# Reordering the seams between the stages of a decoder layer on one core: first loads, table turns, the last stores of y, and who reads y

## What is computed

```python
u = rmsnorm(x, g_mix) @ w_in                     # 1024 -> 512, 32 groups of 16 channels
bu = einsum(u, bb)                               # complex, 64 states a group
s_t = lb * s_(t-1) + bu_t                        # scan over the tokens; samples start from s0
y = gelu(Re(C s) + d * u)                        # 512 wide
a = y @ w_out;  x2 = x + a[:, :1024] * sigmoid(a[:, 1024:])
h = rmsnorm(x2, g_ffn)                           # router: best of 4 groups, then 2 of its 4 experts
x3 = x2 + sum_k weight_k * (silu(h @ w_gate_k) * (h @ w_up_k)) @ w_down_k
out = rmsnorm(x3, g_final), the last state of each sequence
```

## Time and profile before

| | us |
|---|---|
| median of 3 runs (lowest, highest) | 881.96 (881.44, 885.02) |
| the profiled execution's own time | 882.48 |
| its span on the core | 880.7 |
| TensorE busy | 805.5 (91%) |
| VectorE busy | 598.2 (68%) |
| ScalarE busy | 409.0 (46%) |
| PoolE busy | 332.6 (38%) |

### The profile page before, as it was taken

One profiled execution on the slowest core, in us unless ns is written; L12 is line 12 of the kernel. 1 busy time (PEld: TensorE's weight loads), 2 busy tenths in 40 slices (PEclk: granted clock), 3 DMA queues, 4 the chain that ended last, 5 costly groups with the idle time before them and its releaser, 6 DMA issues.

```text
span 880.7 us, 14971 instructions
## 1 busy us (share of the span) xinstructions
PE 805.5 (91%) x4204; PEld 649.6 (74%) x4204; DVE 598.2 (68%) x1143; ACT 409.0 (46%) x737; POOL 332.6 (38%) x443
## 2 busy tenths in 40 slices
PE   4899998996899999999964999999999999999982
PEld 2788875555788888888743788888888888888861
DVE  5798769996333345535575678876867878876852
ACT  6456752123332443424221565764745755754630
POOL 3600001001200000060335257767777667766532
PEclk9899999999899999999975999999999999999996
DMA  7454314886842332423314857865877668876721
GB/s 241 159 212 171 143 18 100 244 179 127 299 144 94 121 137 79 144 93 125 109 26 131 318 207 259 262 231 190 281 250 250 225 232 302 282 254 221 283 90 74
DMA packets 57780, 160.93 MB, mean 183 GB/s; under 512 B 22480, under 2 KB 26960, under 8 KB 51024
## 3 DMA queue, kind: packets, MB, share of 16 engines
q1 hardware_dynamic: 34704, 112.70, 39.6%
q0 software_dynamic: 22976, 47.05, 15.1%
HBM read 128.75 MB, written 62.40 MB: 217 GB/s over the span
## 4 chain that ended last, share of the span: by engine, by line
PE 75%; DMA 7%; DVE 7%; issue 4%; SPq 2%; ACT 1%; POOL 1%; DVEq 0%; POOLq 0%; ACTq 0%
PE pbig L1219 8%; PE pbig L1215 8%; PE pbig L1216 8%; PE pbig L1125 7%; PE pbig L1127 6%; PE pbig L1126 6%; PE pbig L1240 4%; PE pbig L1242 4%; PE pbig L1241 4%; PE pbig L1203 4%; PE pbig L986 3%; PE pbig L988 3%; PE pbig L987 3%; PE pbig L1148 3%; DMA y_by_block<-U 3%
## 5 line engine op out<-in xcount | busy, mean ns | idle before, releaser
L1215 PE MATMUL pbig<-WH,xgH 128*128 x320 | 130.4, 407 | 1.4 <-ACT xgH L885 1.4
L1216 PE MATMUL pbig<-WL,xgH 128*128 x320 | 126.0, 394 | 0.0
L1125 PE MATMUL pbig<-w2H,ysH 128*128 128x512 f32 (+1 forms) x272 | 111.2, 409 | 8.5 <-DVE ysL L1545 8.5
L1127 PE MATMUL pbig<-w2H,ysL 128*128 128x512 f32 (+1 forms) x272 | 108.4, 399 | 0.0
L1126 PE MATMUL pbig<-w2L,ysH 128*128 128x512 f32 (+1 forms) x272 | 108.2, 398 | 0.0
L589 POOL DMA_INDIRECT x_sums<-xg,recs x36 | 81.9, 2276 | 39.3 <-DVE xg L1802 31.6
L1691 DVE SCALAR_TENSOR_TENSOR WL<-WR,gf_p,WH 128x512 f32 (+1 forms) x128 | 86.3, 746 | 5.0 <-ACT WH L851 3.1
L1581 DVE TENSOR_TENSOR x<-pbig,sg 128x1024 f32<-128x1024 f32 (+1 forms) x17 | 20.8, 1224 | 91.6 <-PE pbig L1127 91.2
L851 ACT ACTIVATE WH<-WR,gf_p 128x512 f32 (+1 forms) x128 | 80.5, 711 | 5.2 <-DMA WR<-in_w_gu 3.1
L1219 PE MATMUL pbig<-WH,xgL 128*128 x320 | 81.2, 395 | 0.0
L1802 DVE SCALAR_TENSOR_TENSOR xg<-pbig,recs,xg 128x1024 f32<-128x1024 f32 x40 | 51.2, 1281 | 34.6 <-PE pbig L1242 34.6
(11 more groups left out here) (287 smaller groups left out, 1741.8 us busy)
## 6 DMA issues: line engine op xcount, KB each, us to landing
WR<-in_w_gu SPq DMA_DIRECT2D x32, 1024.0 KB, 6.6
WR<-in_w_dn SPq DMA_DIRECT2D x16, 1024.0 KB, 6.0
xT<-in_x_cols SPq DMA_DIRECT2D x16, 512.0 KB, 3.5
low<-in_x_rows SPq DMA_DIRECT2D x16, 512.0 KB, 4.5
U<-in_x_rows SPq DMA_DIRECT2D x16, 512.0 KB, 5.1
x_mid<-x SPq DMA_DIRECT2D x16, 512.0 KB, 2.6
x_sums<-x SPq DMA_DIRECT2D x16, 512.0 KB, 3.9
w<-in_w_out SPq DMA_DIRECT2D x1, 4096.0 KB, 12.4
```

The source lines that it names most:

```text
L1125: pe.matmul(pbig[0:rows, n, :], ysH[b][:, k, 0:rows], w2H[n][:, k, :], start=(k == 0), stop=False)
L1127: mm = pe.matmul(pbig[0:rows, n, :], ysL[b][:, k, 0:rows], w2H[n][:, k, :], start=False, stop=(k == CB - 1))
L1215: pe.matmul(pbig[:, 6, :], xgH[b][:, k, :], WH[:, w], start=(k == 0), stop=False)
L1216: pe.matmul(pbig[:, 6, :], xgH[b][:, k, :], WL[:, w], start=False, stop=False)
```

## The change

The diff does six things. (1) The loads of the second and third `xT` come ahead of three small tables and of the first rows; ScalarE does `x_root(t)` in step t and not one step earlier; the eight small transfers of the samples are split four and four behind tiles 4 and 5, `a_spread(0)` moves from behind tile 2 to behind tile 6, and the tables `turn_table(5)` and `e_table` swap places. (2) The turns of `E` come three, three and two behind tiles 13, 14 and 15, over four banks. (3) The first two `b_state` go between the last fills, and ScalarE empties all of these but one. (4) The samples' states: ScalarE copies the raw values per step (`fo_raw`), VectorE adds all start states once behind the stage. (5) The stores and loads of the last quarter of y are issued crosswise, each store with its own semaphore. (6) `ys` and PoolE's copies are gone: ScalarE and VectorE read `U` and `ytail`; ScalarE's order of `w2_hi(3)` and `c_y_hi(0, 0)` changes.

```diff
             for k in range(KD):
                 sp.dma_start(w1[:, k, :], w_in[:, k, :]).then_inc(S[f"win{k}"], 16)
+            x_load(1)
             for dst_, src in ((BC[:, :, :, :], bc_in), (s0_sb[:, :, :, :], s0), (d_sb[:, :], d_in)):
                 sp.dma_start(dst_, src).then_inc(S["bc_in"], 16)
+            x_load(2)
             row_load(0)
-            x_load(1)
             row_load(1)
             sp.dma_start(gf_p[:, :], gffn).then_inc(S["rt_in"], 16)
             sp.dma_start(wr_sb[:, :, :], w_route).then_inc(S["rt_in"], 16)
             for t in range(2, TA):
-                x_load(t)
+                if t >= 3:
+                    x_load(t)
                 row_load(t)
-                if t == 2:
+                if t in (4, 5):
 
                     sp.wait_ge(S["us_done"], 1)
-                    for j in range(L):
+                    for j in range(4 * t - 16, 4 * t - 12):
                         sp.dma_start(us8[:, :, L - 1 - j, :], us[j * DECB:(j + 1) * DECB, :, 0, :]).then_inc(S["us8_in"], 16)
...
             cb = CB - 1
-            for q in range(4):
+
+            def tail_store(q):
                 sp.wait_ge(S["gelu_done"], 8 * cb + 2 * q + 2)
-                sp.dma_start(yD[cb][:, 2 * q:2 * q + 2, :], U[:, cb * 8 + 2 * q:cb * 8 + 2 * q + 2, :]).then_inc(S["y_stored"], 16)
-                if q == 0:
-                    sp.wait_ge(S["tabs_ready"], 1)
-                    sp.wait_ge(S["wt_small"], 1)
-                    sp.wait_ge(S["k_done"], 1)
-                sp.wait_ge(S["y_stored"], 16 * (cb + q + 1))
+                sp.dma_start(yD[cb][:, 2 * q:2 * q + 2, :], U[:, cb * 8 + 2 * q:cb * 8 + 2 * q + 2, :]).then_inc(S[f"yt_st{q}"], 16)
+
+            def tail_load(q):
+                sp.wait_ge(S[f"yt_st{q}"], 16)
                 for g in (2 * q, 2 * q + 1):
                     sp.dma_start(ytail[g * GC:(g + 1) * GC, :, :],
                                  yD[cb].rearrange("(i c) g k -> g c i k", c=GC)[g]).then_inc(S["y_tail"], 16)
+
+            tail_store(0)
+            tail_store(1)
+            sp.wait_ge(S["tabs_ready"], 1)
+            sp.wait_ge(S["wt_small"], 1)
+            sp.wait_ge(S["k_done"], 1)
+            tail_load(0)
+            tail_store(2)
+            tail_load(1)
+            tail_store(3)
+            tail_load(2)
+            tail_load(3)
             sp.wait_ge(S["fo_done"], 2 * PR)
+            sp.wait_ge(S["fo_sum"], 1)
             sp.dma_start(st_out, FO[:, :, :, :]).then_inc(S["st_stored"], 16)
...
-            def c_copy(t, part):
...
-                    pool.tensor_copy(ys[b][:, 0:CB - 1, 0:rows], yflat[:, 0:CB - 1, t * P:t * P + rows]).then_inc(S["ys_done"], 1)
...
             x_hi(1)
-            x_root(0)
-            x_root(1)
             for t in range(TA):
                 if 1 <= t < TA - 1:
                     x_hi(t + 1)
-                    x_root(t + 1)
-                if t == 3:
+                x_root(t)
+                if t == 7:
                     spread(0)
                 if t in (L + 2, L + 3):
...
                 if t > TURN_AT:
-                    turned(2 * (t - 1 - TURN_AT))
-                    turned(2 * (t - 1 - TURN_AT) + 1)
+                    for f in range(3 * (t - 1 - TURN_AT), min(3 * (t - TURN_AT), PR // 2)):
+                        turned(f)
             x_scale(TA - 1)
-            turned(PR // 2 - 2)
-            turned(PR // 2 - 1)
-            for q in range(10, FILLS, 2):
+            for q in range(10, FILLS):
                 spread(q)
...
             def c_y_hi(t, part):
                 b, rows = t % 2, P if t < TF else LAST
-                act.wait_ge(S["ys_done"], 2 * t + part + 1)
+                if t == 0 and part == 0:
+                    act.wait_ge(S["y_in"], 16 * (CB - 1) * 8)
+                if t == 0 and part == 1:
+                    act.wait_ge(S["y_tail"], 16 * 8)
+                if t == 1 and part == 0:
+                    act.wait_ge(S["fo_sum"], 1)
...
-                k = slice(0, CB - 1) if part == 0 else slice(CB - 1, CB)
-                act.activation(ysH[b][:, k, 0:rows], ys[b][:, k, 0:rows], ACT.Copy).then_inc(S["ys_hi"], 1)
+                if part == 0:
+                    act.activation(ysH[b][:, 0:CB - 1, 0:rows], yflat[:, 0:CB - 1, t * P:t * P + rows], ACT.Copy).then_inc(S["ys_hi"], 1)
+                else:
+                    act.activation(ysH[b][:, CB - 1, 0:rows], ylast[:, t * P:t * P + rows], ACT.Copy).then_inc(S["ys_hi"], 1)
...
+            def fo_raw(r):
+                act.wait_ge(S["rot_done"], 2 * r + 2)
+                act.activation(FO[:, :, r, 0:DECB], pbig[:, 2 * (r % 2):2 * (r % 2) + 2, 0:DECB], ACT.Copy).then_inc(S["fo_raw"], 1)
+
+            fo_raw(0)
+            fo_raw(1)
             for r in range(PR - 2):
                 b_gelu(r)
                 if r + SB < PR:
                     act.wait_ge(S["y_done"], 2 * r + 2)
                     b_head(r + SB)
+                fo_raw(r + 2)
             act.wait_ge(S["wout_in"], 16)
             act.wait_ge(S["v_done"], PR)
             w2_hi(2)
             b_gelu(PR - 2)
+            c_y_hi(0, 0)
             act.wait_ge(S["turned_on"], 2 * PR)
-            w2_hi(3)
-            c_y_hi(0, 0)
             b_gelu(PR - 1)
             act.wait_ge(S["y_done"], G)
+            w2_hi(3)
             w2_hi(0)
             w2_hi(1)
...
                 if f == 0:
                     pe.wait_ge(S["e_ready"], 1)
+                    pe.wait_ge(S["ue_act"], 9)
+                if f == 2:
                     pe.wait_ge(S["k_evac"], G // 4)
-                if f >= 2:
-                    pe.wait_ge(S["et_evac"], f - 1)
-                bank = pbig[:, 6 + f % 2, :]
+                if f >= 4:
+                    pe.wait_ge(S["et_evac"], f - 3)
+                bank = pbig[:, 4 + f % 4, :]
...
-                if t == 2:
+                if t == 6:
                     a_spread(0)
...
                 if t >= TURN_AT:
-                    e_spread(2 * (t - TURN_AT))
-                    e_spread(2 * (t - TURN_AT) + 1)
-            for q in range(9, FILLS):
-                a_spread(q)
+                    for f in range(3 * (t - TURN_AT), min(3 * (t - TURN_AT) + 3, PR // 2)):
+                        e_spread(f)
...
-                if r % 2 == 0:
-                    q = 9 + r // 2
-                    pe.wait_ge(S["ue_dve" if q % 2 else "ue_act"], (q - 7) // 2 if q % 2 else 9 + (q - 8) // 2)
+                    pe.wait_ge(S["ue_dve"], 1)
+                if r % 2 == 0 and r >= 2:
+                    pe.wait_ge(S["ue_act"], 9 + r // 2)
                 if r >= 2:
-                    pe.wait_ge(S["v_used"], r - 1)
+                    pe.wait_ge(S["rot_done"], 2 * r - 2)
+                    pe.wait_ge(S["fo_raw"], r - 1)
...
+            for q in range(9, 12):
+                a_spread(q)
             b_state(0)
+            a_spread(12)
             b_state(1)
+            for q in range(13, FILLS):
+                a_spread(q)
             for r in range(PR):
                 if r + 2 < PR:
                     b_state(r + 2)
                 b_out(r)
 
 
-            pe.wait_ge(S["v_used"], PR)
+            pe.wait_ge(S["rot_done"], 2 * PR)
+            pe.wait_ge(S["fo_raw"], PR)
...
-                if t == 10:
+                if t == 6:
                     dve.wait_ge(S["wt_small"], 1)
                     for im in range(2):
                         turn_table(5, im)
+                if 7 <= t < 11:
+                    if t == 7:
+                        dve.wait_ge(S["tr_done"], 1)
+                    e_table(*divmod(t - 7, 2))
...
-                if t + 1 < TA:
-                    x_factor(t + 1)
-            for q in range(9, FILLS, 2):
-                spread(q)
+                x_factor(t)
+            spread(9)
...
                     dve.wait_ge(S["z_done"], 2 * r)
                 tt(r1[b][:, :, :], v, turns(r)[0], ALU.mult).then_inc(S["rot_done"], 1)
                 tt(r2[:, :, :], v, turns(r)[1], ALU.mult).then_inc(S["rot_done"], 1)
-                tt(FO[:, :, r, 0:DECB], pbig[:, 2 * b:2 * b + 2, 0:DECB], F0[:, :, r, :], ALU.add).then_inc(S["v_used"], 1)
...
             dve.wait_ge(S["fo_done"], 2 * PR)
             w2_lo(2)
             c_y_lo(0, 0)
+            dve.wait_ge(S["fo_raw"], PR)
+            tt(FO[:, :, :, 0:DECB], FO[:, :, :, 0:DECB], F0[:, :, :, :], ALU.add).then_inc(S["fo_sum"], 1)
+            dve.wait_ge(S["fo_sum"], 1)
             w2_lo(3)
             w2_lo(0)
             w2_lo(1)
```

More of the change, by code:

```diff
@@ L387, in c_store @@
                     sp.dma_start(xD[t * P:t * P + rows, :], cut(x2[b], rows)[:, :]).then_inc(S[f"x2_st{b}"], 16)
+            for q in range(4):
+                sp.wait_ge(S[f"yt_st{q}"], 16)
             c_load(0)
@@ L1073, in b_out @@
                 if r == 0:
[L1074 to L1075 removed]
+                    pe.wait_ge(S["ue_act"], 16)
                 if r % 4 == 0:
@@ L1543, in c_y_lo @@
```

(5 more changed lines are left out.)

59 lines of the change are left out of this document (13 added, 46 removed).

## The result

The changed kernel takes 869.4 us (median of 4 runs, 867.84 to 872.65) against 882.74 for the kernel before on the same chip: ratio 0.9851, 95% interval 0.9815 to 0.9887. In two later groups the same kernel gave 0.9848 (0.9824 to 0.9872) and 0.9844 (0.9821 to 0.9868). Forecast were 867.2 and a range of 863.8 to 873.5. The profiled execution is the slowest of the four: own time 872.65, span 870.6.

A forecast was written before the change was run, and what follows sets the result against it. TensorE bounds mid-stage A and stage C, VectorE paces stage B. Earlier starts at the seams bring stage C's tile 1 forward by 14.8 us: 882.48 - 14.8 = 867.7, 867.2 as a median; range 863.8 to 873.5.

The forecast's parts named there:

- rival 1: The forecast itself for the whole kernel, 865 to 870 us; chance 0.64.
- Opening, 7.1: Stage A's opening: tile 3 starts at 32.1 at full clock and ends 7.1 us earlier; bounds 5 and 8.5.
- Fill 0, 2.1 lost: Stage A: fill 0, moved from a gap of TensorE to behind tile 6 without one, loses 2.1 us.
- E's turns, 0: End of stage A: turns moved ahead of tile 16 gain nothing for the fills, which start at 120.7.
- Rotation 0: Start of stage B: VectorE's first rotation no longer waits for all eight fills and comes at 123.7.
- `b_state(2)`: Start of stage B: waits for ScalarE's raw copy until 129.6; rotation 2 at 131.2 against 137.60, 6.4 us earlier.
- Body, 1.0: Stage B's steps: VectorE sheds the sum into `FO`, 0.08 a step over 13 steps, 1.0 us gained.
- w_out, 7.5: SyncE's queue before stage C: w_out's load issued at 142.1 instead of 149.58, y moving with it; bound only 4.0.
- First tile and last quarter: Stage C starts at 197.9, y's last quarter reaches TensorE at 209.8, tile 1 at 213.5 against 228.25, 14.8 us earlier.
- ScalarE's table switch: Opening, on ScalarE: 1.28 us, root directly behind it; by the skill's 2.66 the sum would be about 868.6.
- lower bound of the last quarter: Last quarter of y: eight loads in a row, 9.8, and two more stores, 1.6, give 208.3.
- rival 2: Last quarter of y keeps its rounds of stores and loads, tile 1 at 220.4, 874 us; chance 0.12.

The follow-up runs named there:

- after_again: The changed kernel once more, unaltered, on another chip: 869.76 us, ratio 0.9848 to the kernel before.
- u_open: The changed kernel with its opening undone (loads, squares and roots, tables, small transfers and fill 0 as before): 874.1 us, ratio 0.9897 to the kernel before.
- u_sum: The changed kernel with VectorE adding the start states in each step again, without ScalarE's raw copies: 868.39 us, ratio 0.9838 to the kernel before.
- u_tail: The changed kernel with y's last quarter in rounds again (store, wait, two loads, four times): 885.65 us, ratio 0.9948 to the kernel before.
- i_raw: The changed kernel with ScalarE's raw copies of steps 0 and 1 ahead of `CLn`: 868.96 us, ratio 0.9856 to the kernel before.
- i_wout: The changed kernel with w_out's load issued ahead of `T`'s last two quarters: 878.09 us, ratio 0.9861 to the kernel before.

## Why the prediction was nearly right, point by point

The time was 2.2 above the forecast and in its range; it is rival 1 (865 to 870). The seam steps behind y's landing were exact, the two ahead of it too large. By its own trace the forecast was further off than the median says: tile 1 came 10.7 earlier where 14.8 were forecast. In after_again, whose profiled execution is its median (869.76), tile 1 is at 215.53, 12.7 earlier, though on another chip. So some 2 us of the shortfall belong to the execution that was profiled, and that the time came so near is in part luck.

- **Opening, 7.1.** `x_first` landed at 19.5 as worked out, and tile 3 started at 32.37 against 32.1. The step that failed is "tile 3 then runs at full clock, 5.4": it took 7.16 behind two waits of 2.60 and 1.97, so the term measured 5.05, my own lower bound of 5. In other profiles the clock held and VectorE was slow beside PoolE instead. I had taken VectorE's durations from a trace in which PoolE's instructions over 256 elements lay in VectorE's idle 5 us. Both in the kernel before:

```profile
32.30 0.62 POOL L445 TENSOR_TENSOR WT<-WT,tabs 128x256 f32<-128x256 f32 x1
```

```profile
36.21 1.23 DVE L1320 TENSOR_TENSOR xL<-xT,xH 128x1024 fp32r<-128x1024 f32 x1 [5.09 <-ACT xH L667]
```

- **Fill 0, 2.1 lost.** Right (2.07), with a rider: in 7 of the 12 profiles that have it behind tile 6, the clock falls in the next tile, 1.6 us more.
- **E's turns, 0.** Right: 0.93 idle ahead of the fills against 0.94. The fills came at 123.04, not 120.7.
- **Rotation 0.** Offset from the fills 2.75 against 3.0. **`b_state(2)`**: right place, right releaser; it came 9.34 behind the fills instead of 8.9, and the half clock behind the wait, 0.5 more until rotation 2, was not in the sum. Rotation 2 is 3.1 earlier, not 6.4: 2.3 of the difference is stage A's, 1 this. By rotation 3 the half clock has cost 1.2 (16.2 behind the first fill against 15.0 in u_open). From the first fill to the start of the last rotation it is 68.5 instead of 69.6, 1.1 less where 2.4 were forecast, and 69.9 in after_again, where the clock is down through most of the first output: no gain at all.
- **Body, 1.0.** The step is 4.37 (139.22 to 143.59) against 4.44. But the price of the raw copies at the start is as large: undoing them is no loss (u_sum).
- **w_out, 7.5.** It moved 4.3: 1.8 for `T`'s start (123.23 in the trace against 125.00, where 4.0 were forecast), 2.5 for the wait, since the 32 issues take 22.0 us without it. That this queue is the limit was right, and stronger than I used it: from w_out's issue to y's split it was 54.7 to 55.8 in all nine profiles with w_out behind `T` and no copy, whatever stage B did. In the same nine the third store was issued 37.6 to 41.1 behind w_out and landed 44.3 to 45.5 behind it. Moving w_out or stage B alone gives 1.2 to 2.5 by the profiles and nothing clear in the time, both together 3.7 to 4.9.
- **First tile and last quarter.** From the landing of y to the last quarter's split 12.3 as forecast (208.9 - 196.6), to tile 1 16.5 against 16.9. The rounds' cost was real: u_tail. That the 12.3 is exact is luck in part: it was picked between 11.4 and 17.5, and 11.4 rests on eight loads in a row, while these go out in four groups from 201.6 to 210.1. TensorE had no gap ahead of the last 12 matmuls and did them at full clock, which is the 0.4. The figure of the Trainium skill that stands beside this step (DMA: Bandwidth & Descriptors, "Anatomy of one DMA") is given there for transfers that PoolE issues, and y's loads are SyncE's; these loads took 3.7 to land here, in the median, as in the row, and not 2.3.
- **ScalarE's table switch.** 1.28 us and the root directly behind it (20.71, then 22.00). The Trainium skill (ScalarE: Activation LUTs, "What ACT_TABLE_LOAD costs") has a drain behind it; this trace again shows none.

So 14.8 at tile 1 became 10.7: 2.2 since stage A ended late, 1.0 in `T`'s issues (22.0 against 24.54 - 3.5 = 21.0) and 1.2 between w_out's issue and y (55.8 against 54.6), less 0.4 at the end. In u_tail, i_raw and i_wout the parts could be moved one by one; that stage A and the queue add up in this way is read from the traces.

Two slips of the prediction changed nothing. The lower bound of the last quarter counts from 196.9 where its own sum gives 196.6. And rival 2's time, 874, lies above the range's end of 873.5, so the range doesn't hold most of that rival, as the prediction says, but less than half.

## What to carry to other kernels

Where two chains meet at a seam, removing a wait from one can show little or nothing in the time until the other is moved too: change both before you judge either, and look for the interval that stays constant over all versions. When work is moved, ask which engine it will now run beside, not only which queue it stands in: durations taken from a trace in which the neighbour was idle don't hold. And put a small copy that frees a buffer ahead of the long instructions in its queue.
